# Reading the moving operand of split float32 products from the last column to the first, in a two-layer decoder trunk

## The chip, the cores and the metric

The kernel runs on one core of a Trainium2 chip. The metric is device time in microseconds; each number for a kernel is the median of several runs. Before the change: 1374.74 us, median of 3 runs (1374.43 to 1375.49).

## The reference

What is computed is a decoder trunk of two residual layers on 256 tokens of width 1024, all in float32:

```python
# layer 0
p = rms_norm(x) @ w_in_ab                 # 1024 x 2816
x = x + concat([gmlp(p), dilated_attention(p)]) @ w_out_ab
x = x + swiglu(rms_norm(x), ffn_w_gate, ffn_w_up, ffn_w_down)      # width 2816
# layer 1
p = rms_norm(x) @ w_in_cd                 # 1024 x 3072
x = x + concat([moba_attention(p), short_conv(p)]) @ w_out_cd
# 8 experts of width 3584; each token has two of them
h = rms_norm(x)
x = x + sum(gate[..., e] * (silu(h @ wg[e]) * (h @ wu[e])) @ wd[e] for e in range(8))
```

Nearly all of the arithmetic is in the products with the weight matrices: the projections, the dense feed-forward and the eight experts.

## The kernel before, in words

**Split products.** TensorE multiplies operands of the type `float32r`, a rounded float32. To keep more of the precision, every operand of a large product is split into two such parts: hi is the rounded value, lo is the remainder, rounded too. A product is then three matmuls into the same PSUM bank: hi x hi, hi x lo and lo x hi. The helper `three` (lines 786 to 790) issues them. Its arguments are the output in PSUM, the stationary operand (`sh`, `sl`: hi and lo) and the moving operand (`mh_`, `ml_`). TensorE first loads the stationary operand (128 x 128) and then streams the columns of the moving operand through the array, one after the other, and each gives one column of the result.

**Weights.** A stream of weight tiles of 2 MB comes from HBM into a ring of seven slots (`raw_ring`), loaded by SyncE's queue. Each tile is worked on in four units of 128 x 1024 values. For a unit ScalarE makes the hi part (`w_hi`, lines 402 and 423), VectorE makes the lo part (`w_lo`, lines 410 and 428), and TensorE uses both. There are four buffers for units (`SPLITS`). The semaphores `hi_ready`, `lo_ready` and `unit_used` count units: ScalarE waits for TensorE to have used a unit four before, VectorE waits for ScalarE, and TensorE waits for VectorE.

**Order of the work.** Every engine's program is written out by hand in order. TensorE's begins with the projection of layer 0 (`first_tile`, `project`), then attention with the output projection (`attention`, `ab_unit`), the dense feed-forward (`ffn`, `down`), the projection and the attention of layer 1 (`project`, `c_attention`, `conv_half`, `out_first`, `out_units`, `out_last`), the routing, and then the experts in `job`. A job is one expert on up to 128 gathered tokens: 21 steps of a gate, an up or a down tile, each of four units, and each unit is six matmuls of 512 columns. The first job stands alone, and the others are the passes of a loop.

**The two shapes.** In most places the activations are stationary and the weights move: the moving operand is a row of `w_hi` or `w_lo` of 512 columns (256 where a tile is narrower), and the output is a whole bank or half of one. In the dense feed-forward from its second slab on, and in the convolution (`conv_half`), the weights are stationary and 256 columns of activations (`ffn_in_hi`, `act_hi` and their lo parts) move.

Transposes, the small attention products and the gathers of tokens call TensorE directly and don't go through the helper.

Of the kernel before, what the change touches and what calls it, by code (L numbers as in the profile page):

```python
# [174 lines left out]
def decoder_trunk(nc, x, norm_mix, norm_ffn, w_in_ab, gmlp_v_gain, gmlp_ws, gmlp_bs, dil_q_gain, dil_k_gain,  # L175
# [10 lines left out]
    with ExitStack() as ctx:  # L186
# [4 lines left out]
        def at(name, shape, dt, offset):  # L191
            return nc.alloc_sbuf_tensor_at(name, [P, *shape], dt, offset=offset)
# [77 lines left out]
        mh = at("moe_h", [2, SLAB], F32, R0 + 12288)  # L270
# [111 lines left out]
        def raw_unit(u):  # L382
            t, r0, n, c0, w = units[u]
            _, nrow, ncol = tiles[t]
            full = raw[:, t % RING, 0:nrow * ncol].rearrange("p (k f) -> p k f", f=ncol)
            return full[:, r0:r0 + n, c0:c0 + w]
# [4 lines left out]
        def split_hi(act, u):  # L391

            if u >= U_MOE:
                return
            t, _, _, _, w = units[u]
            if u < 3:
                act.wait_ge(quarter_loaded[u], 16)
            else:
                act.wait_ge(slot_loaded[t % RING], 16 * (t // RING + 1))
            if u >= SPLITS:  # L400
                act.wait_ge(unit_used, u - SPLITS + 1)
            act.activation(part(wh, u, w), raw_unit(u), ACT.Copy).then_inc(hi_ready, 1)  # L402
# [380 lines left out]

        @block.tensor
        def _(pe):
            def three(out_, sh, sl, mh_, ml_, start, stop):

                pe.matmul(out_, sh, mh_, start=start, stop=False)  # L788
                pe.matmul(out_, sh, ml_, start=False, stop=False)  # L789
                return pe.matmul(out_, sl, mh_, start=False, stop=stop)  # L790

            def setup_mix():
                pe.wait_ge(ident_loaded, 16)
# [30 lines left out]
            def first_tile(n, u0, later_rows):  # L824

                for tt in range(TT):
                    sl = slice(tt * P, tt * P + P)
                    for i in range(4):
                        u = u0 + i
                        _, r0, cnt, _, w = units[u]  # L830
                        if tt == 0:
                            pe.wait_ge(lo_ready, u + 1)
                        pe.wait_ge(xt_lo, 8 * n + 4 * tt + i + 1)
                        for r in range(cnt):
                            k = r0 + r
                            mm = three(ps[:, tt, 0:w], in_hi[n][:, k, sl], in_lo[n][:, k, sl],
                                       part(wh, u, w)[:, r, :], part(wl, u, w)[:, r, :], k == 0, k == KD - 1)
                        if tt == 1:
                            mm.then_inc(unit_used, 1)
                        if tt == 0 and i == later_rows:  # L840
                            x_T(n, 1, 0)
                            x_T(n, 1, 1)
# [7 lines left out]
            def project(u0, u1, layer, c0=0):  # L850

                u, c = u0, c0
                while u < u1:
                    t = units[u][0]
                    ncol = tiles[t][2]
                    b = (c % 2) * 2
                    if c == 1 and layer == 0:
                        setup_columns()
                        setup_rows()
                        setup_ws()  # L860
                    if c == 2 and layer == 1:
                        spread_scale(2)
                    if c >= 2:
                        pe.wait_ge(proj_act, read_act[layer][c - 2])
                    while u < u1 and units[u][0] == t:
                        _, r0, n, _, w = units[u]
                        pe.wait_ge(lo_ready, u + 1)
                        for r in range(n):
                            k = r0 + r
                            for tt in range(TT):  # L870
                                sl = slice(tt * P, tt * P + P)
                                mm = three(ps[:, b + tt, 0:ncol], act_hi[:, k, sl], act_lo[:, k, sl],
                                           part(wh, u, w)[:, r, :], part(wl, u, w)[:, r, :], k == 0, k == KD - 1)
                        mm.then_inc(unit_used, 1)
                        u += 1
                    c += 1
# [190 lines left out]
            def conv_half(n):  # L1067

                i, half = divmod(n, 2)
                z, c = divmod(i, 2)  # L1070
                u = first["conv"] + i
                if half == 0:
                    pe.wait_ge(lo_ready, u + 1)
                    if i == 0:
                        pe.wait_ge(proj_act, 11)
                    if i == 4:
                        pe.wait_ge(cv_z, 1)
                o = ps[:, CONV_BANK[z], c * SEQ:(c + 1) * SEQ]
                for k in range(4 * half, 4 * half + 4):
                    mm = three(o, part(wh, u, P)[:, k, :], part(wl, u, P)[:, k, :],  # L1080
                               act_hi[:, k, :], act_lo[:, k, :], k == 0, k == KD - 1)
                if half == 1:
                    mm.then_inc(unit_used, 1)
# [328 lines left out]
            for half in range(2):  # L1412
# [5 lines left out]
                for t in range(TT):  # L1418
                    pe.matmul(bank(QUARTER_BANKS[half * TT + t]), pick_t[:, t, :], y_lo[:, cs],
                              start=False, stop=True).then_inc(last_done, 1)  # L1420
# [1191 lines left out]
```

## Time and profile before

| what | value |
|---|---|
| median of 3 runs | 1374.74 us |
| span of the profiled execution | 1372.6 us |
| TensorE busy | 1354.2 us, 6885 matmuls |
| TensorE weight loads | 1139.1 us, beside the matmuls |
| VectorE busy | 1180.1 us |
| ScalarE busy | 1017.8 us |
| moved by DMA | 430.89 MB |

The profiled execution is one of its own. Its time is given as the span, from its first to its last instruction; the medians of the runs also hold what lies around that. A matmul's row in the trace begins when it begins to stream and ends when its last result is modelled to have arrived, so rows of matmuls that follow each other overlap, and the time that one takes from the next is the distance between their starts. The granted clock (PEclk) is the share of TensorE's full clock of 2.4 GHz: 1.00 is that level, 0.50 would be 1.2 GHz.

### The profile page before, as it was taken

What the parts mean: (1) busy time and instruction counts of PE and PEld (TensorE: products, weight loads), DVE (VectorE), ACT (ScalarE), POOL (GpSimd) and SP (SyncE); (2) the same over time, 40 slices, a digit from 0 to 9 for tenths busy, and PEclk for the clock granted to TensorE, in tenths of its full rate; (3) what the DMA queues carried; (4) which work ended last, traced back from release to release, by engine and by line L of the source; (5) the groups of instructions that cost most, each with busy time, mean ns of one, the idle gap of its engine ahead of it and who ended that gap; (6) DMA issues with size and microseconds to landing.
All of it is one profiled execution on the core that took longest, in us unless ns stands there. A gap on an engine that the chain in (4) does not pass through costs nothing.

```text
span 1372.6 us, 19885 instructions
## 1 busy us (share of the span) xinstructions
PE 1354.2 (99%) x6885; PEld 1139.1 (83%) x6885; DVE 1180.1 (86%) x1369; ACT 1017.8 (74%) x1189; POOL 133.2 (10%) x132
## 2 busy tenths in 40 slices
PE   9999999999998999999999999999999999999998
PEld 7778999988987788888888888888888888888886
DVE  5876555568959999999999999999999999999998
ACT  5656444456757778888888888888888888888886
POOL 1020000000222240200200110020020002003000
PEclk9999999999999999999999999999999999999999
DMA  9944543643656999999999999999999999999980
GB/s 346 361 144 162 184 154 123 229 139 123 246 217 254 363 373 372 383 395 375 369 394 397 354 391 398 369 372 394 392 354 391 400 368 371 395 387 356 394 335 31
DMA packets 184623, 430.89 MB, mean 314 GB/s; under 512 B 6076, under 2 KB 14032, under 8 KB 184576
## 3 DMA queue, kind: packets, MB, share of 16 engines
q1 hardware_dynamic: 181136, 422.81, 82.8%
q0 software_dynamic: 3440, 7.44, 2.5%
q8 instruction: 30, 0.49, 0.1%
q14 instruction: 17, 0.14, 0.0%
HBM read 425.68 MB, written 7.36 MB: 315 GB/s over the span
## 4 chain that ended last, share of the span: by engine, by line
PE 90%; DVE 6%; DMA 1%; issue 1%; ACT 1%; POOL 0%; DVEq 0%; SPq 0%; POOLq 0%; ACTq 0%
PE psum L788 29%; PE psum L790 28%; PE psum L789 28%; DVE w_lo L428 2%; PE psum L1360 2%; DVE w_lo L410 1%; DMA slot_table<-routing,table_row 1%; DMA routing<-slot_table 0%; PE psum L820 0%; PE psum L921 0%; POOL slot_table L712 0%; DVE probs L2114 0%; PE psum L1062 0%; DMA const<-const_f 0%; PE psum L953 0%
## 5 line engine op out<-in xcount | busy, mean ns | idle before, releaser
L428 DVE TENSOR_TENSOR w_lo<-raw_ring,w_hi 128x1024 fp32r<-128x1024 f32 x674 | 811.2, 1228 | 49.0 <-ACT w_hi L423 12.1
L423 ACT ACTIVATE w_hi<-raw_ring 128x1024 fp32r<-128x1024 f32 x675 | 713.1, 1062 | 169.3 <-PE psum L790 168.4
L788 PE MATMUL psum<-w_hi,xg_hi 128*128 128x512 f32 x896 | 351.4, 392 | 4.2 <-DVE w_lo L428 4.1
L790 PE MATMUL psum<-w_hi,xg_lo 128*128 128x512 f32 x896 | 349.0, 390 | 0.0
L789 PE MATMUL psum<-w_lo,xg_hi 128*128 128x512 f32 x896 | 348.7, 389 | 0.0
L410 DVE TENSOR_TENSOR w_lo<-raw_ring,w_hi 128x1024 fp32r<-128x1024 f32 x124 | 151.3, 1227 | 78.0 <-ACT w_hi L402 77.1
L788 PEld LDWEIGHTS psum<-w_hi,xg_hi 128*128 128x128 f32 x896 | 168.2, 188 | 40.0 <-DVE w_lo L428 4.1
L402 ACT ACTIVATE w_hi<-raw_ring 128x1024 fp32r<-128x1024 f32 x124 | 130.0, 1058 | 93.9 <-PE psum L790 93.6
L790 PEld LDWEIGHTS psum<-w_hi,xg_lo 128*128 128x128 f32 x896 | 168.2, 188 | 35.4
L789 PEld LDWEIGHTS psum<-w_lo,xg_hi 128*128 128x128 f32 x896 | 168.3, 188 | 34.1
L788 PE MATMUL psum<-w_hi,moe_hT_hi 128*128 128x512 f32 x448 | 175.7, 392 | 0.7 <-DVE w_lo L428 0.7
L790 PE MATMUL psum<-w_hi,moe_hT_lo 128*128 128x512 f32 x448 | 174.5, 390 | 0.0
L789 PE MATMUL psum<-w_lo,moe_hT_hi 128*128 128x512 f32 x448 | 174.4, 389 | 0.0
L788 PEld LDWEIGHTS psum<-w_hi,moe_hT_hi 128*128 128x128 f32 x448 | 84.1, 188 | 19.8 <-issue 1.4
L790 PEld LDWEIGHTS psum<-w_hi,moe_hT_lo 128*128 128x128 f32 x448 | 84.1, 188 | 17.8
L789 PEld LDWEIGHTS psum<-w_lo,moe_hT_hi 128*128 128x128 f32 x448 | 84.1, 188 | 16.9
L788 PE MATMUL psum<-w_hi,act_hi 128*128 128x512 f32 (+1 forms) x224 | 86.0, 384 | 2.9 <-DVE w_lo L410 1.9
L789 PE MATMUL psum<-w_lo,act_hi 128*128 128x512 f32 (+1 forms) x224 | 83.9, 375 | 0.0
L790 PE MATMUL psum<-w_hi,act_lo 128*128 128x512 f32 (+1 forms) x224 | 83.9, 375 | 0.0
L788 PE MATMUL psum<-ffn_in_hi,w_hi 128*128 128x256 f32 x288 | 80.9, 281 | 0.0
L789 PE MATMUL psum<-ffn_in_lo,w_hi 128*128 128x256 f32 x288 | 80.6, 280 | 0.0
L790 PE MATMUL psum<-ffn_in_hi,w_lo 128*128 128x256 f32 x288 | 80.6, 280 | 0.0
(299 smaller groups left out, 1348.4 us busy)
## 6 DMA issues: line engine op xcount, KB each, us to landing
raw_ring<-in_moe_w_gate SPq DMA_DIRECT2D x56, 2048.0 KB, 10.4
raw_ring<-in_moe_w_up SPq DMA_DIRECT2D x56, 2048.0 KB, 11.0
raw_ring<-in_moe_w_down SPq DMA_DIRECT2D x56, 2048.0 KB, 10.1
raw_ring<-in_ffn_w_gate SPq DMA_DIRECT2D x5, 2048.0 KB, 12.5
raw_ring<-in_ffn_w_up SPq DMA_DIRECT2D x5, 2048.0 KB, 8.9
raw_ring<-in_ffn_w_down SPq DMA_DIRECT2D x5, 2048.0 KB, 10.3
raw_ring<-in_w_in_ab SPq DMA_DIRECT2D x4, 2048.0 KB, 19.4
raw_ring<-in_w_in_cd SPq DMA_DIRECT2D x4, 2048.0 KB, 8.0
```

Source lines behind the costliest of these rows:

```text
L402: act.activation(part(wh, u, w), raw_unit(u), ACT.Copy).then_inc(hi_ready, 1)
L410: dve.tensor_tensor(part(wl, u, w), raw_unit(u), part(wh, u, w).bitcast(F32), ALU.subtract).then_inc(lo_ready, 1)
L423: act.activation(wh[:, v % SPLITS, :], moe_raw(i, q), ACT.Copy).then_inc(hi_ready, 1)
L428: dve.tensor_tensor(wl[:, v % SPLITS, :], moe_raw(i, q), wh[:, v % SPLITS, :].bitcast(F32), ALU.subtract).then_inc(lo_ready, 1)
L788: pe.matmul(out_, sh, mh_, start=start, stop=False)
L789: pe.matmul(out_, sh, ml_, start=False, stop=False)
L790: return pe.matmul(out_, sl, mh_, start=False, stop=stop)
L1360: mm = pe.transpose(ps[:, 4 + n % 2, c * P:(c + 1) * P], mh[:, n % 2, c * P:(c + 1) * P], ident)
```

## The change

In the helper of the split products the output and both parts of the moving operand are turned: the access pattern begins at the last column and goes down by one column at a time. Column n of the moving operand still gives column n of the output, so the result is the same; only the order in which columns are read and written differs. The stationary operands are not touched.

```diff
+            def turned(v):
+
+                return v[:, v.shape[-1] - 1::-1]
+
             def three(out_, sh, sl, mh_, ml_, start, stop):
 
-                pe.matmul(out_, sh, mh_, start=start, stop=False)
-                pe.matmul(out_, sh, ml_, start=False, stop=False)
-                return pe.matmul(out_, sl, mh_, start=False, stop=stop)
+                o, mh, ml = turned(out_), turned(mh_), turned(ml_)
+                pe.matmul(o, sh, mh, start=start, stop=False)
+                pe.matmul(o, sh, ml, start=False, stop=False)
+                return pe.matmul(o, sl, mh, start=False, stop=stop)
```

The instructions of all five engines stand in the same order as before; after the change the helper's three matmuls are lines 793 to 795, and the lines below are five further on.

## Rows read from the trace of the kernel before

**Rows 1.** The page's head, busy time by engine, and its slices.

```profile
span 1372.6 us, 19885 instructions
PE 1354.2 (99%) x6885; PEld 1139.1 (83%) x6885; DVE 1180.1 (86%) x1369; ACT 1017.8 (74%) x1189; POOL 133.2 (10%) x132
...
PEclk9999999999999999999999999999999999999999
```

**Rows 2.** The page's chain that ended last, by engine and line.

```profile
PE 90%; DVE 6%; DMA 1%; issue 1%; ACT 1%; POOL 0%; DVEq 0%; SPq 0%; POOLq 0%; ACTq 0%
PE psum L788 29%; PE psum L790 28%; PE psum L789 28%; DVE w_lo L428 2%; PE psum L1360 2%; DVE w_lo L410 1%; DMA slot_table<-routing,table_row 1%; DMA routing<-slot_table 0%; PE psum L820 0%; PE psum L921 0%; POOL slot_table L712 0%; DVE probs L2114 0%; PE psum L1062 0%; DMA const<-const_f 0%; PE psum L953 0%
```

**Rows 3.** Busy time by engine in one pass of the expert loop.

```profile
core 0: us, PE busy (x) PEld busy (x) DVE busy (x) ACT busy (x) POOL busy (x), PEclk, DMA share, GB/s
754.41:871.97 117.56, 117.56 (x535) 97.40 (x533) 110.63 (x100) 96.74 (x99) 9.87 (x9) 1.00 1.03 382
```

**Rows 4.** Waits of TensorE: total us, times, longest; the first two.

```profile
PE psum L788 <- DVE w_lo L428: 4.8, 5, 1.7
PE psum L788 <- DVE w_lo L410: 1.9, 4, 0.6
```

**Rows 5.** TensorE's groups by form, line 788: busy us, mean ns.

```profile
L788 PE MATMUL psum<-w_hi,xg_hi 128*128 128x512 f32 x896 | 351.4, 392 | 4.2 <-DVE w_lo L428 4.1
...
L788 PE MATMUL psum<-w_hi,moe_hT_hi 128*128 128x512 f32 x448 | 175.7, 392 | 0.7 <-DVE w_lo L428 0.7
...
L788 PE MATMUL psum<-ffn_in_hi,w_hi 128*128 128x256 f32 x288 | 80.9, 281 | 0.0
...
L788 PE MATMUL psum<-w_hi,act_hi 128*128 128x512 f32 x192 | 76.7, 399 | 2.9 <-DVE w_lo L410 1.9 <-issue 0.8
...
L788 PE MATMUL psum<-w_hi,ffn_h_hi 128*128 128x512 f32 x88 | 34.4, 391 | 0.0
...
L788 PE MATMUL psum<-act_hi,w_hi 128*128 128x256 f32 x48 | 14.5, 303 | 0.2 <-ACT p_v L1709 0.2
...
L788 PE MATMUL psum<-w_hi,ffn_in_hi 128*128 128x512 f32 x32 | 12.8, 399 | 0.2 <-DVE ffn_in_lo L1916 0.2
...
L788 PE MATMUL psum<-w_hi,act_hi 128*128 128x256 f32 x32 | 9.3, 290 | 0.0
```

**Rows 6.** Timeline of TensorE in the experts, 512 columns: start us, us.

```profile
799.95 0.39 PE L788 MATMUL psum<-w_hi,xg_hi 128*128 128x512 f32 x1
...
804.02 0.39 PE L788 MATMUL psum<-w_hi,xg_hi 128*128 128x512 f32 x1
```

**Rows 7.** Timeline of TensorE in the dense feed-forward, 256 columns.

```profile
179.84 0.28 PE L788 MATMUL psum<-ffn_in_hi,w_hi 128*128 128x256 f32 x1
...
181.96 0.28 PE L788 MATMUL psum<-ffn_in_hi,w_hi 128*128 128x256 f32 x1
```

**Rows 8.** Line 1342: its rows in the timeline, and one's duration (min/median/max ns).

```profile
410.48 1.02 PE L1342 MATMUL psum<-const 128*128 128x512 f32 x2
...
L1342 PE MATMUL psum<-const x2: 592/594/595, 410.5 to 410.9; 128*128 128x512 f32 x2
```

## The prediction
> **What bounds the kernel now.** I read the head of the page first. TensorE is busy for 1354.2 of 1372.6 us and its granted clock is at full share in every slice, so the engine runs at the 2.4 GHz level from end to end [rows 1]. The profiled execution has its span alone as a time; the median of the three runs is 1374.74 us, 2.1 us above it, and I put those 2.1 us around the span both before and after. Next the chain of waits: 90% of it is TensorE, and 29 + 28 + 28 = 85% of the span lies on three lines, 788 to 790, which are the body of `three`, the helper that the change edits [rows 2]. Then I ask whether something else is close behind. In one pass of the expert loop (117.56 us) TensorE has no idle time; VectorE is busy for 110.63 us and ScalarE for 96.74 us [rows 3]. The longest waits of TensorE on the whole span are 4.8 and 1.9 us [rows 4]. So a matmul that gets slower lengthens the run almost one for one, and one that gets faster shortens it until VectorE's 110.63 us per pass is reached.
>
> How many matmuls does the edit touch, and at what pace do they run? The groups by form give the counts for line 788 [rows 5]; lines 789 and 790 have the same counts. With 512 columns: 896 + 448 + 192 + 88 + 32 = 1656 per line, 4968 on the three. With 256 columns: 288 + 48 + 32 = 368 per line, 1104 on the three. Together 6072 of the 6885 matmul rows. The mean of one in that view (392 ns) is not the pace, because a matmul's row overlaps the next one's. The pace is read from starts in the timeline: from 799.95 to 804.02 us there are 18 matmuls of 512 columns, so 4.07/18 = 0.2261 us each [rows 6]; from 179.84 to 181.96 us there are 18 of 256 columns, 2.12/18 = 0.1178 us each [rows 7]. The difference, 0.1083 us for 256 columns, is 0.423 ns per column, and one clock at 2.4 GHz is 0.417 ns. So a column goes through in one clock, and what is left is a fixed 0.2261 - 512 x 0.000423 = 9.5 ns per matmul. All in all 4968 x 0.2261 + 1104 x 0.1178 = 1123 + 130 = 1253 us, 91% of the span.
>
> **The change part by part.** It removes no instruction, adds none and moves none: each engine's program holds the same rows in the same order, and only the two operands' address patterns differ. The step from column to column becomes -1 and the start becomes the last column. The stationary operand is read as before, so weight loads stay as they are. Waits and signals sit on the same matmuls. Each output column still receives the same products in the same sequence of matmuls. A bank's reader still waits for the end of the last matmul of its group, so it does not matter to it which column was written last. Within a group every matmul is turned, so a given column is returned to one matmul later, as before. Work that does not go through the helper (transposes, attention products, gathers, 813 rows) is untouched. All these parts cost 0 us, and no cover is needed for any of them.
>
> What is left is one unknown: the price of stepping backwards, for the read of the moving operand and for the write of the result. No matmul of the kernel before has a negative step on either side, so I bound the price.
>
> *From above.* The nearest row in which TensorE takes more time per column is line 1342, a plain float32 product of 512 columns done in two passes. From its start at 410.48 us to the end of the second pass are 1.02 us, and one pass shows 0.594 us, so the second began 0.426 us after the first [rows 8]. That is 0.83 ns per column, two clocks instead of one at the same granted clock. If a backward step cost this, a product of 512 columns would take 0.426 - 0.2261 = 0.200 us more, and one of 256 (half of 0.426 is 0.213) 0.0952 us more: 4968 x 0.1999 + 1104 x 0.0952 = 993 + 105 = 1098 us.
>
> *From below.* The stream is already at one column per clock, so the columns themselves can't go faster. At most the fixed 9.5 ns could vanish: 6072 x 9.5 ns = 58 us. In one pass (21 steps of four units of six matmuls, 504) that would be 4.8 us, less than the 117.56 - 110.63 = 6.9 us by which VectorE is shorter, so VectorE would not stop it.
>
> Between ends so far apart I take 0. What the row of line 1342 has different is the kind of product (plain float32 in two passes), not the order of addresses: its operands are read forwards. The turned products are of the same kind, width and alignment as the rows at 0.2261 us; they touch the same bytes of the same banks, all of them and each once, and have the same number of columns per matmul. An even width turned round pairs the same neighbours: 511 with 510 instead of 510 with 511.
>
> The Trainium skill speaks on both sides here. "PSUM — Partial Sum Buffer", section Specifications (TRN2), says that PSUM has lines of 8 bytes and that any non-contiguous access pattern slows matmuls significantly. "SBUF — State Buffer", section on the DMA port swizzle, says that SBUF lines are 16 bytes and that consecutive accesses to the same line run at full bandwidth. If a step of -1 counts as non-contiguous, the first makes the sum the rival's below; if only staying in the line counts, it makes the sum 0, since two float32 columns share an 8-byte line and four share a 16-byte line in either direction. No run here shows yet which reading holds.
>
> The sum is 0 us on a median of 1374.74: I predict 1374.7 us. For this kernel, with three runs spread over 1.06 us, I call a difference under 0.2% (2.75 us) no change.
>
> **The rivals.** (1) *Backwards at half the rate.* TensorE streams two columns at a time only upwards, or merges pairs of writes only upwards, and falls to two clocks per column. The place is the moving read or the PSUM write of all 6072 matmuls, the price is the 1098 us above, and the time 1374.7 + 1098 = 2473 us. For it: line 1342 shows that the engine has such a rate [rows 8]. Against it: the same bytes, the same pairs. It decides as soon as a matmul costs 0.45 ns more (2.75 us over 6072), since TensorE has next to no slack [rows 3, 4]. Chance 0.09. (2) *A fixed price per matmul*, for instance a start in the middle of a line: between 0.45 ns and once more the fixed 9.5 ns, so up to 6072 x 9.5 ns = 58 us and at most 1432 us; one extra clock alone would be 2.5 us, or 1377.3. Nothing speaks for it but that the starting address is another one. Chance 0.05. (3) *Faster*: part of the fixed 9.5 ns goes, or the read meets the accesses of the other engines less often; 1317 us at the utmost. Against it: the pace is the same 0.2261 us while VectorE and ScalarE are busy for 94% and 82% of the time, and it is already one column per clock but for that remainder. Chance 0.03. (4) *The change doesn't reach the chip*, because the two reversals are folded into a forward pattern: the built program holds the step of -1 on both operands, so I give it no chance apart from the forecast's, with which it shares its time.
>
> **How the numbers follow.** Forecast 0.83, rivals 0.09, 0.05 and 0.03. Faster by over 0.2% is rival 3: 0.03. Slower by over 0.2% is rivals 1 and 2: 0.14. Within 0.2%: 0.83. The forecast's own band is 1372.0 to 1377.5 us. I carry the upper end to 1380, which takes in two extra clocks per matmul (6072 x 0.83 ns = 5.1 us), the cheap part of rival 2; rival 1 is left out, because nothing lies between.
>
> **What would show it.** If right: starts of consecutive 512-column products stay 0.226 us apart and those of 256 columns 0.118 us, the three lines of the helper keep about 85% of the chain, one pass of the expert loop stays at 117.6 us, and ScalarE still ends its waits on TensorE. If rival 1 holds, the starts are 0.43 us apart, VectorE's share falls to nearly half, and the loop's pass takes over 210 us. If rival 2 holds, both widths are longer by the same number of nanoseconds. A different spacing of the starts for 512 and 256 columns, or a granted clock below full share, would prove the argument wrong even at the same total.

## The result, and the profile after

The changed kernel takes 1402.82 us (median of 4 runs, 1402.51 to 1403.27) against 1374.59 us for the kernel before (median of 4, one more than before the prediction): ratio 1.0204, 95% interval 1.0189 to 1.0218. It is slower by 28.2 us. The forecast was no change, with a range up to 1380 us.

The head of the page of the changed kernel, its slices of the granted clock, and its chain by line:

```profile
span 1401.4 us, 19885 instructions
PE 1385.1 (99%) x6885; PEld 1142.2 (82%) x6885; DVE 1183.3 (84%) x1369; ACT 1017.6 (73%) x1189; POOL 118.6 (8%) x132
...
PEclk9999999999999999999999999999999999999999
...
PE psum L793 30%; PE psum L795 29%; PE psum L794 29%; PE psum L1365 2%; DVE w_lo L428 1%; DVE w_lo L410 1%; PE psum L825 0%; PE psum L1224 0%; PE psum L926 0%; DVE probs L2119 0%; PE psum L1067 0%; PE psum L958 0%; DVE rope_tmp L480 0%; DVE p_qk L482 0%; PE psum L1218 0%
```

Against [rows 1, 2]: the same instructions, the same clock, the same three lines on the chain. TensorE is busy for 30.9 us more (1385.1 - 1354.2), and its idle time falls from 18.4 to 16.3 us, since some waits for VectorE shrink: 30.9 - 2.1 = 28.8 us, the growth of the span. One pass of the expert loop, the counterpart of [rows 3]:

```profile
core 0: us, PE busy (x) PEld busy (x) DVE busy (x) ACT busy (x) POOL busy (x), PEclk, DMA share, GB/s
646.52:767.21 120.69, 120.69 (x534) 97.63 (x533) 111.01 (x100) 96.70 (x99) 8.63 (x9) 1.00 1.01 372
```

It is 3.13 us longer, 6.2 ns for each of its 504 products. VectorE and ScalarE need what they needed. The starts of products in TensorE's timeline, as in [rows 6, 7], first the 512 columns of the experts, then the 256 columns of the dense feed-forward:

```profile
822.45 0.40 PE L793 MATMUL psum<-w_hi,xg_hi 128*128 128x512 f32 x1
...
826.65 0.40 PE L793 MATMUL psum<-w_hi,moe_hT_hi 128*128 128x512 f32 x1
...
179.92 0.28 PE L793 MATMUL psum<-ffn_in_hi,w_hi 128*128 128x256 f32 x1
...
182.04 0.28 PE L793 MATMUL psum<-ffn_in_hi,w_hi 128*128 128x256 f32 x1
```

Between each pair lie 18 products: 4.20/18 = 0.2333 us with 512 columns (0.2261 before), and 2.12/18 = 0.1178 us with 256 (0.1178 before). These two windows alone would say 7.2 ns for 512 columns; the pass averages over 504 products, and I go by its 6.2 ns. So the whole price lies on the 4968 products of 512 columns, and at 6.2 ns each it is 30.8 us.

### The profile page after: what moved, and what is told of

The parts are those of the page before. It is cut to its first block, busy times and chain, and to the rows that moved or that the text cites. A ratio compares the mean times of both kernels' runs of the same rounds, so it can differ in the third digit from the quotient of the medians.

```text
span 1401.4 us, 19885 instructions
## 1 busy us (share of the span) xinstructions
PE 1385.1 (99%) x6885; PEld 1142.2 (82%) x6885; DVE 1183.3 (84%) x1369; ACT 1017.6 (73%) x1189; POOL 118.6 (8%) x132
## 4 chain that ended last, share of the span: by engine, by line
PE 93%; DVE 5%; ACT 1%; issue 1%; DVEq 0%; ACTq 0%
PE psum L793 30%; PE psum L795 29%; PE psum L794 29%; PE psum L1365 2%; DVE w_lo L428 1%; DVE w_lo L410 1%; PE psum L825 0%; PE psum L1224 0%; PE psum L926 0%; DVE probs L2119 0%; PE psum L1067 0%; PE psum L958 0%; DVE rope_tmp L480 0%; DVE p_qk L482 0%; PE psum L1218 0%
## 5 line engine op out<-in xcount | busy, mean ns | idle before, releaser
L793 PE MATMUL psum<-w_hi,xg_hi 128*128 128x512 f32 x896 | 358.4, 400 | 3.7 <-DVE w_lo L428 3.6
L794 PE MATMUL psum<-w_lo,xg_hi 128*128 128x512 f32 x896 | 356.2, 398 | 0.0
L795 PE MATMUL psum<-w_hi,xg_lo 128*128 128x512 f32 x896 | 356.0, 397 | 0.0
L793 PE MATMUL psum<-w_hi,moe_hT_hi 128*128 128x512 f32 x448 | 178.8, 399 | 0.1
L795 PE MATMUL psum<-w_hi,moe_hT_lo 128*128 128x512 f32 x448 | 178.0, 397 | 0.0
L794 PE MATMUL psum<-w_lo,moe_hT_hi 128*128 128x512 f32 x448 | 178.0, 397 | 0.0
```

The costliest lines, as they stand in the source:

```text
L793: pe.matmul(o, sh, mh, start=start, stop=False)
L794: pe.matmul(o, sh, ml, start=False, stop=False)
L795: return pe.matmul(o, sl, mh, start=False, stop=stop)
```

## The experiments

Five of the twelve runs are tables of extra products: rows of 24 matmuls of one kind, on a source line each, behind the last matmul of the kernel before, while the other engines rest (VectorE's last products and the last transfers end within the first row). They write PSUM banks that nobody reads any more. What counts there is the distance between starts within a row; I give it as the start of the next row minus the start of this one, over 24. Their whole times (1475 to 1499 us) say nothing.

### Read or write, and which width

```diff
...
+            for n in R:
+                pe.matmul(o5, wt, m5, start=n == 0, stop=n == 23)
+            for n in R:
+                pe.matmul(back(o5), wt, back(m5), start=n == 0, stop=n == 23)
+            for n in R:
+                pe.matmul(o5, wt, back(m5), start=n == 0, stop=n == 23)
+            for n in R:
+                pe.matmul(back(o5), wt, m5, start=n == 0, stop=n == 23)
...
```

> The kernel before with rows of 24 extra products behind its last matmul (they write PSUM banks whose contents are not needed any more), so the time grows by some 110 us and only the distance between starts within each row counts. In the kernels before and after that distance is 226.7 and 233.3 ns for 512 columns, and 117 and 118 ns for 256. Theory 1, the READ of the moving operand backwards costs time per column: both turned and read turned give 233 at 512 columns, write turned alone 227; 384 columns get 5 ns longer and 256 columns 3 ns unless something else (the weight load) already holds 256 columns at 117. Theory 2, the WRITE to PSUM backwards costs time: both and write turned give 233, read turned alone 227. Theory 3, a fixed price per matmul at its start: +6.6 ns at every width that is not held by the weight load, so 384 columns too. Theory 4, the moving reads meet the reads of the next weight load, which is done beside them: the price shrinks with the number of stationary columns, so with 64 or 32 of them both directions fall towards 213 ns (512 columns at one per clock) and their difference vanishes; under theories 1 to 3 it stays. If the other engines' accesses were the cause, the directions would not differ here, since they rest. Single products without accumulation and two alternating banks: no change under any of these. Reads that start at column 1 or 2 tell whether the start within a line matters.

The timeline of the extra rows (start us, us in all, line). Line 1431 reads and writes 512 columns forwards, 1433 turns both, 1435 the read alone, 1437 the write alone; 1439 and 1441 are 384 columns, 1443 and 1445 are 256, forwards and with both turned:

```profile
1368.11 5.60 PE L1431 MATMUL psum<-moe_y_hi,pick_T 128*128 128x512 f32 x24
1373.55 5.77 PE L1433 MATMUL psum<-moe_y_hi,pick_T 128*128 128x512 f32 x24
1379.15 5.76 PE L1435 MATMUL psum<-moe_y_hi,pick_T 128*128 128x512 f32 x24
1384.75 5.62 PE L1437 MATMUL psum<-moe_y_hi,pick_T 128*128 128x512 f32 x24
1390.21 4.35 PE L1439 MATMUL psum<-moe_y_hi,pick_T 128*128 128x384 f32 x24
1394.40 4.42 PE L1441 MATMUL psum<-moe_y_hi,pick_T 128*128 128x384 f32 x24
1398.66 3.04 PE L1443 MATMUL psum<-moe_y_hi,pick_T 128*128 128x256 f32 x24
1401.54 3.01 PE L1445 MATMUL psum<-moe_y_hi,pick_T 128*128 128x256 f32 x24
1404.38 5.63 PE L1447 MATMUL psum<-moe_y_hi,pick_T 128*128 128x512 f32 x24
```

Forwards (1373.55 - 1368.11)/24 = 226.7 ns, both turned 233.3, read turned 233.3, write turned 227.5. So it is the read. 384 columns: 174.6 and 177.5; 256 columns: 120.0 and 118.3. The two numbers of the kernel come back with the other engines at rest, so they have no part in it. Products that don't accumulate, further down in the table, gave 227.9 and 233.3, so accumulation has none either. Theories 2 and 3 fall. Theory 4 in its plain form falls as well: with 64 and 32 stationary columns the forward rows took 230.0 and 231.3 and the backward ones 233.8 and 233.3, no nearer to 213. One thing fitted nothing: forward reads from column 1 and 2 took 237.5 and 233.3 ns, as slow as backward ones.

### Widths, starts and order in blocks

The same frame with other rows: more widths, other first columns, and the 512 columns in blocks of 4, 16 or 256.

```diff
...
+                pe.matmul(o4, wt, by4[:, 127::-1, :], start=n == 0, stop=n == 23)
...
+                pe.matmul(o4, wt, by4[:, :, 3::-1], start=n == 0, stop=n == 23)
...
```

> The kernel before with rows of 24 extra products behind its last matmul; only the distance between starts within a row counts. All write forwards except where a block pattern says so. Theory A (the backward read has a slower rate): 227.7, 174.5, 120.0 ns forwards and 233.3, 177.6, 118.7 backwards for 512, 384, 256 columns lie on lines of 0.42 ns per column + 13 and 0.45 + 4. So 448 columns: 200 and 205; 320: 147 and 148; 192 and 128: 93 and 67 forwards, 90 and 61 backwards, or the floor of a weight load (about 109) if that is longer, and then no difference. Theory B (a fixed price at the first column of a backward read, which 256 columns hide behind the weight load): 448 and 320 columns both get 6.6 ns longer. Start of a read: a forward read from column 2 took 233.2, from column 1 237.7; if lines of 16 bytes matter, 4, 8 and 16 are back at 227 and 3 is not; if 32 or 64 bytes matter, only 8 or 16 are. Backward from 515, 519 or 527 shows the same from the other end (233 or better). Blocks: if the order of the lines costs, blocks of 4 or 16 columns read from the last block to the first, each forwards, take 233 and blocks in order that are turned inside take 227; if the order inside a line costs, the other way round.

Lines 1441 and 1443 are 320 columns forwards and backwards; 1453 and 1455 are 512 columns forwards from column 8 and 16; 1467 reads blocks of 4 columns from the last to the first, 1469 blocks in order but each turned inside:

```profile
1378.51 3.71 PE L1441 MATMUL psum<-moe_y_hi,pick_T 128*128 128x320 f32 x24
1382.06 3.69 PE L1443 MATMUL psum<-moe_y_hi,pick_T 128*128 128x320 f32 x24
1385.58 5.04 PE L1445 MATMUL psum<-moe_y_hi,pick_T 128*128 128x448 f32 x24
...
1406.48 5.76 PE L1453 MATMUL psum<-moe_y_hi,pick_T 128*128 128x512 f32 x24
1412.08 5.67 PE L1455 MATMUL psum<-moe_y_hi,pick_T 128*128 128x512 f32 x24
1417.59 6.00 PE L1457 MATMUL psum<-moe_y_hi,pick_T 128*128 128x512 f32 x24
...
1445.91 5.76 PE L1467 MATMUL psum<-moe_y_hi,pick_T 128*128 128x512 f32 x24
1451.51 5.63 PE L1469 MATMUL psum<-moe_y_hi,pick_T 128*128 128x512 f32 x24
1456.97 5.76 PE L1471 MATMUL psum<-moe_y_hi,pick_T 128*128 128x512 f32 x24
```

| columns | 128 | 192 | 256 | 320 | 384 | 448 | 512 |
|---|---|---|---|---|---|---|---|
| forwards, ns | 109.6 | 113.3 | 120.0 | 147.9 | 174.6 | 203.3 | 226.7 |
| backwards, ns | 111.3 | 111.3 | 118.3 | 146.7 | 177.5 | 206.7 | 233.3 |

(256, 384 and 512 are from the first table, where both operands are turned.) Up to 320 columns the two directions differ by about 2 ns at most, now one way and now the other; at 384 and 448 backwards costs about 3 ns and at 512 it costs 6.6. That is neither a slower rate per column nor a fixed price, so theory A and theory B are both wrong in form. Blocks of 4 columns (16 bytes) in reverse order cost the full price, 233.3; the same blocks in order but turned inside cost nothing, 227.5. So it is the order in which the 16-byte pieces follow each other that counts, not the order inside one. Two blocks of 256 in reverse order, each read forwards, took 228.8: one step back in the middle costs next to nothing. Blocks of 16 turned inside were the slowest of the rows in blocks, 266.7. A read that alternates between forwards and backwards from one product to the next took 236.3, and one backwards from column 514 took 242.9; the runs leave both unexplained. And forward reads that start 8 columns on took 233.3, from 16 on 229.6: the *place* of a forward read matters as much as the direction.

### In the kernel: only 256 columns, only the read, only the write

```diff
...
+                if out_.shape[-1] == 256:
+                    out_, mh_, ml_ = turned(out_), turned(mh_), turned(ml_)
```

> The helper turns its operands only where the output has 256 columns (1104 of 6072 matmuls). Theory A (slower rate, with 256 columns held by something else, as the 120.0 and 118.7 ns of the extra rows show): no change, 1374 to 1376 us. Theory B (a fixed price per matmul): 1104 x 6.6 ns = 7.3 us more, 1382 us.

Measured 1375.27 us (ratio 1.0005, interval 0.9995 to 1.0014): no change, as the table of widths says.

For the next two, the gate and up products of the experts alone are touched, and the two readers of their banks read backwards, so that the result stays right:

```diff
...
-                                mm = three(bank(b), xg_hi[:, k, :], xg_lo[:, k, :], wh[:, w % SPLITS, cs],
-                                           wl[:, w % SPLITS, cs], k == 0, k == KD - 1)
+                                mm = three(bank(b), xg_hi[:, k, :], xg_lo[:, k, :], turned(wh[:, w % SPLITS, cs]),
+                                           turned(wl[:, w % SPLITS, cs]), k == 0, k == KD - 1)
...
-                        act.activation(msg[:, i % 2, :], bank(i % 2), ACT.Silu).then_inc(silu_ready, 1)
+                        act.activation(msg[:, i % 2, :], bank(i % 2)[:, 511::-1], ACT.Silu).then_inc(silu_ready, 1)
...
-                dve.tensor_tensor(mh[:, i % 2, :], msg[:, i % 2, :], bank(2 + i % 2), ALU.mult).then_inc(h_ready, 1)
+                dve.tensor_tensor(mh[:, i % 2, :], msg[:, i % 2, :], bank(2 + i % 2)[:, 511::-1], ALU.mult).then_inc(h_ready, 1)
```

> Only the experts' gate and up products (2688 matmuls of 512 columns), and only the moving operand read backwards; the bank is written forwards, so it holds the columns in reverse, and the two readers (ScalarE's silu, VectorE's product) read it backwards. Theory A (the read is what costs): 2688 x 6.6 ns = 17.7 us more, 1392 us. Rival (the write costs in the loaded loop): no change, 1375 us.

Measured 1390.52 us (ratio 1.0117, interval 1.0100 to 1.0134), 16.0 us more, against 2688 x 6.2 = 16.7 us at the price per product of the result. TensorE's timeline where a down step, read forwards, goes over into a gate step, read backwards:

```profile
820.43 0.39 PE L792 MATMUL psum<-w_hi,moe_hT_hi 128*128 128x512 f32 x1
...
822.47 0.40 PE L792 MATMUL psum<-w_hi,xg_hi 128*128 128x512 f32 x1
...
824.57 0.40 PE L792 MATMUL psum<-w_hi,xg_hi 128*128 128x512 f32 x1
```

Nine products lie between each two: (822.47 - 820.43)/9 = 226.7 ns, then (824.57 - 822.47)/9 = 233.3 ns.

With `turned(bank(b))` in place of the two `turned(wh...)` and `turned(wl...)`:

> The same gate and up products, but only the output is written backwards; the moving operand is read forwards, and the same two readers read the bank backwards. Theory A: no change, 1374 to 1376 us. Rival (the write costs in the loaded loop): 1392 us. If the readers' reversed reads cost ScalarE or VectorE time, this and the run with the backward read show it alike in the mean durations of the silu and of the product (680 ns before).

Measured 1374.65 us (ratio 1.0000, interval 0.9991 to 1.0010). Writing backwards is free, in the loaded loop too. Reading a bank backwards is free for ScalarE and VectorE: the product of silu and up took 681 ns in the mean, as against 680 before, and the silu 579 as against 581.

### The place of the stationary operand

The forward reads with another start left a new question. In every table the stationary operand stayed where it was while the moving one went on. Now the stationary operand moves within its buffer `y_lo`. Its place is the column of `y_lo` at which it begins; `y_lo` itself begins 12288 bytes, 48 x 256, behind `y_hi`, so place 0 is a multiple of 256 bytes from the moving operand's first column:

```diff
...
+                pe.matmul(o5, y_lo[:, 8:136], y_hi[:, 0:512], start=n == 0, stop=n == 23)
...
+                pe.matmul(o5, y_lo[:, 8:136], back(y_hi[:, 0:512]), start=n == 0, stop=n == 23)
...
```

> The kernel before with rows of 24 extra products of 512 columns behind its last matmul, all written forwards. So far the extra rows with the stationary operand in one place gave 227 (forwards from column 0), 233 (backwards from column 511), and forwards from column 2, 4, 8, 16: 233.2, 231.8, 233.2, 229.3, so a forward read can cost as much as a backward one. Theory C: the moving read and the read of the next stationary operand, which goes on beside it, meet in SBUF, and what counts is where one lies against the other and in which directions they go. Then moving the stationary operand alone, by 2 to 128 columns, changes the forward pace from 227 in the same way (231 to 235 for some), a common shift of both by 4, 8 or 16 columns gives 227 again, and the backward pace varies with it too and is 227 or so for some place. Theory D: the moving read alone sets the pace, by its own start and direction. Then moving the stationary operand changes nothing (227 forwards, 233 backwards in every row), a common shift keeps 231.8, 233.2 and 229.3, and shifts of the moving read by 32 to 256 columns are 227 or slightly more.

Lines 1428 and 1430 have the stationary operand at place 0, 1440 and 1442 at 8, 1452 at 64 columns (the first of each pair reads forwards); 1462 has both operands 8 columns on:

```profile
1368.61 5.60 PE L1428 MATMUL psum<-moe_y_hi,moe_y_lo 128*128 128x512 f32 x24
1374.05 5.77 PE L1430 MATMUL psum<-moe_y_hi,moe_y_lo 128*128 128x512 f32 x24
1379.66 5.71 PE L1432 MATMUL psum<-moe_y_hi,moe_y_lo 128*128 128x512 f32 x24
...
1402.01 5.75 PE L1440 MATMUL psum<-moe_y_hi,moe_y_lo 128*128 128x512 f32 x24
1407.60 5.77 PE L1442 MATMUL psum<-moe_y_hi,moe_y_lo 128*128 128x512 f32 x24
1413.20 5.77 PE L1444 MATMUL psum<-moe_y_hi,moe_y_lo 128*128 128x512 f32 x24
...
1435.68 5.62 PE L1452 MATMUL psum<-moe_y_hi,moe_y_lo 128*128 128x512 f32 x24
1441.13 5.77 PE L1454 MATMUL psum<-moe_y_hi,moe_y_lo 128*128 128x512 f32 x24
...
1463.36 5.63 PE L1462 MATMUL psum<-moe_y_hi,moe_y_lo 128*128 128x512 f32 x24
1468.82 5.63 PE L1464 MATMUL psum<-moe_y_hi,moe_y_lo 128*128 128x512 f32 x24
```

The same forward read takes 226.7 ns with the stationary operand at place 0, 232.9 at place 8, 227.1 at place 64, and 227.5 when both go 8 columns on. Backwards: 233.8, 233.3, 233.3. Theory D falls: the place of the stationary operand sets the pace of a forward read. The load of the stationary operand takes 188 to 189 ns on average in every row of this table, so it is not the load that gets longer. A common shift by 4 columns gave 231.7 where theory C wanted 227, so the rule is not exact below 8 columns.

The remaining places, with two runs of whole kernels beside them:

> The remaining places of the stationary operand in steps of 4 columns (12, 20 to 28, 36 to 60; a shift of 64 gave the same as 0), each with the moving operand read forwards and backwards, 512 columns, behind the last matmul of the kernel before. Theory C, in the form that forwards and backwards each have good and bad places: forwards 229 to 234 except near 0 or 64, backwards 227 or so for at least one place that has not been tried. Theory C2, the backward read meets the stationary read wherever that lies, because both go down through the columns: backwards 233 to 237 everywhere. A place with less than 226.7 in either direction would be one that beats both kernels.

| place of the stationary operand, columns | 0 | 2 | 4 | 8 | 12 | 16 | 20 | 24 | 28 |
|---|---|---|---|---|---|---|---|---|---|
| forwards, ns | 226.7 | 230.8 | 233.3 | 232.9 | 233.3 | 233.8 | 232.1 | 233.8 | 233.3 |
| **place** | **32** | **36** | **40** | **44** | **48** | **52** | **56** | **60** | **64** |
| forwards, ns | 232.5 | 232.9 | 232.9 | 230.4 | 228.8 | 232.1 | 233.3 | 227.9 | 227.1 |

Backwards every place gave 233 to 234, but for 32 and 36, with 236.7 and 237.1. So theory C missed for the backward read: no place tried is a good one. The numbers are those of C2, but its reason is not shown by them, and no run reads the stationary operand in the opposite order, which would test it. For a forward read 0, 60 and 64 are good places. No row was below 226.7, so nothing here beats the kernel before.

The two kernels move the buffers R0 and R1, which hold the stationary operands of the experts, the projections and the down products, by 32 bytes (the constant `PHASE` is added to their address); the moving ones, `w_hi` and `w_lo`, stay:

```diff
-PHASE, FFN_PHASE = 32, -64
+PHASE, FFN_PHASE = 64, -64
```

> The changed kernel with the buffers of activations (the stationary operands of the projections, the experts and the down products) 32 bytes, 8 columns, further on, and the moving ones where they were. The extra rows gave 233.4 ns backwards with this shift and 233.5 without. Theories C and C2: no change against the changed kernel, 1402 to 1404 us. Theory D (the direction alone sets the pace): the same.

The changed kernel with the shift: 1402.95 us, ratio to the kernel before 1.0207 (1.0190 to 1.0224), as without it.

> The kernel before with the same shift of the stationary buffers by 32 bytes; everything is read and written forwards. Theory C: forward products of 512 columns fall to the 233 ns that this shift gave in the extra rows (227 without), so 4968 x 6.3 ns = 31 us less some waits that go, 1400 to 1405 us, as slow as the changed kernel without turning anything. Theory D (direction alone): no change, 1374 to 1376 us.

The kernel before with the shift, nothing turned: 1402.86 us, ratio 1.0209 (1.0192 to 1.0226). It is as slow as the changed kernel. One pass of its expert loop, and its largest group by form:

```profile
646.26:766.88 120.62, 120.62 (x534) 97.54 (x533) 110.94 (x100) 96.77 (x99) 8.53 (x9) 1.00 1.02 374
...
L788 PE MATMUL psum<-w_hi,xg_hi 128*128 128x512 f32 x896 | 356.9, 398 | 3.8 <-DVE w_lo L428 3.7
```

120.62 us for a pass against 117.56 in [rows 3] and 120.69 in the changed kernel. Two more shifts, by `PHASE` of 288 (256 bytes) and of 96 (64 bytes), test the period:

> The kernel before with its buffers of activations 256 bytes (64 columns) further on, all read and written forwards. Theory C (for a forward read only the place of the stationary operand against the moving one counts, and places repeat after 64 columns, as the extra rows with 64 and 128 gave 227.3 and 227.7): no change against the kernel before, 1373 to 1376 us. Rival (any shift of these buffers costs time, through the other engines or by chance): about 1403 us, as with 32 bytes.

> The same with 64 bytes (16 columns). Theory C: the extra row with a shift of 16 columns gave 233.8 ns forwards, 227 without a shift: 1402 to 1406 us. Rival (what counts is the alignment of each buffer to 64 bytes by itself): no change, 1375 us.

256 bytes: 1374.58 us (ratio 0.9999, 0.9989 to 1.0008). 64 bytes: 1404.21 us (ratio 1.0214, 1.0197 to 1.0231). Both as theory C has it. In the kernel before, `w_hi` begins at byte 131200 of each partition and R0 at 186752; the difference, 55552, is 217 x 256, so nearly all of its large products stand at place 0.

The exception is a check within one run. The 96 products of 512 columns with `ffn_in_hi` and `ffn_in_lo` as stationary operands have them 64 bytes below R0 (`FFN_PHASE`), at place 48. The shift by 64 bytes takes these to place 0 and the others to 16. In that run's timeline they alone keep the fast pace, (134.25 - 130.16)/18 = 227.2 ns, while the experts' products take (826.20 - 822.00)/18 = 233.3 ns:

```profile
130.16 0.39 PE L788 MATMUL psum<-w_hi,ffn_in_hi 128*128 128x512 f32 x1
...
134.25 0.39 PE L788 MATMUL psum<-w_hi,ffn_in_hi 128*128 128x512 f32 x1
...
822.00 0.40 PE L788 MATMUL psum<-w_hi,xg_hi 128*128 128x512 f32 x1
...
826.20 0.40 PE L788 MATMUL psum<-w_hi,moe_hT_hi 128*128 128x512 f32 x1
```

### A shorter stationary operand

```diff
...
+                pe.matmul(ps[0:2, 0, 0:512], y_lo[:, 0:2], y_hi[:, 0:512], start=n == 0, stop=n == 23)
...
```

> Extra rows of 24 products behind the last matmul, now with 2 to 96 stationary columns. If what the backward read lacks is a good meeting with the read of the next stationary operand, that read has to matter less as it gets shorter: with 2 or 8 stationary columns both directions and both places (0 and 8 columns further on) come out alike, within 1 ns, at 227 or below, down to 213 if it is all of what lies over one column per clock; with 96 the difference is about that of 128 (227 and 233). Rival: the direction itself or the place costs whatever the length of the stationary read; then 2 columns still show 227 and 233. With 128 stationary columns in the bad place (8 further on): 384 moving columns take about 177 in both directions (173 to 174 forwards in the good place), and 256 columns 118 to 120 in both, which is why those widths showed little or nothing.

Lines 1427 and 1429 have 2 stationary columns, 1447 and 1449 have 96, forwards and backwards:

```profile
1369.22 5.66 PE L1427 MATMUL psum<-moe_y_hi,moe_y_lo 128*2 128x512 f32 x24
1374.71 5.77 PE L1429 MATMUL psum<-moe_y_hi,moe_y_lo 128*2 128x512 f32 x24
1380.32 5.73 PE L1431 MATMUL psum<-moe_y_hi,moe_y_lo 128*8 128x512 f32 x24
...
1424.88 5.69 PE L1447 MATMUL psum<-moe_y_hi,moe_y_lo 128*96 128x512 f32 x24
1430.41 5.77 PE L1449 MATMUL psum<-moe_y_hi,moe_y_lo 128*96 128x512 f32 x24
1436.02 5.72 PE L1451 MATMUL psum<-moe_y_hi,moe_y_lo 128*2 128x512 f32 x24
```

Two columns: 228.8 forwards, 233.8 backwards; 96 columns: 230.4 and 233.8. The expectation missed: a shorter read of the stationary operand does not bring the directions together, and forwards it even loses part of the advantage. With 32 stationary columns at place 8 a forward read took 238.8, more than the backward one beside it (233.8). With 128 stationary columns in the bad place (8), 384 moving columns took 173.8 forwards, no worse than in the good one, and 256 took 118.3. So the place matters at 512 columns and not at these two widths. That the two reads meet in SBUF, as theory C has it, is not shown: what the runs show is that order and place set the pace, and by what mechanism stays open.

## Why the prediction was wrong

**What bounds the kernel: right.** TensorE without slack, the three lines of the helper on the chain, and a full granted clock [rows 1 to 4] all came back in the changed kernel, and the 30.8 us of the products reached the end but for some 2 us of waits.

**That nothing else moves: right.** Same instructions, same busy time of VectorE per pass (110.63 and 111.01 us), and the write side is free (227.5 ns, 1374.65 us).

**The step that failed** is the choice between the bounds: "Between ends so far apart I take 0", on the ground that the turned products touch the same bytes in the same pairs. That counts bytes and leaves out the order in which they are read: blocks of 4 columns in reverse order cost the full price, the same blocks turned inside cost nothing. It also took the rows at 0.2261 us [rows 6] for the rate of a forward read as such. They are the rate of a forward read whose stationary operand lies a multiple of 256 bytes from it; at the other places tried the same read takes 228 to 234 ns, the shifted kernel before takes 1402.86 us, and a backward read has no place among those tried where it does better than 233. The change took that advantage away; by what mechanism the order and the place act is open. The price is 6.2 ns per product of 512 columns, 30.8 us, between my two ends of -58 and +1098 us but far from where I put it.

**A second step was weak:** the split of the pace into 0.423 ns per column and a fixed 9.5 ns, drawn through two widths [rows 6, 7]. In the table of widths 128 and 192 columns cost about the same (110 and 113 ns), and from 320 to 512 columns the line is (226.7 - 147.9)/192 = 0.41 ns per column with 226.7 - 512 x 0.417 = 13 ns left. The products of 256 columns showed no loss when they were turned, and a line through both widths could not show that one of them is insensitive.

**The rivals.** Half the rate was wrong by a factor of about 35 (1098 us forecast, 31 measured). The fixed price per matmul had a span of 1377.5 to 1432 us that holds 1402.8, but its mechanism is wrong: by it both widths had to lengthen by the same time, and 256 columns did not lengthen. The prediction named the sign that would prove it wrong, a different change for 512 and 256 columns, and that is what came.

**The rules of the pages.** The Trainium skill's "PSUM — Partial Sum Buffer", section Specifications (TRN2), warns of non-contiguous access patterns of matmuls; a step of -1 in PSUM cost nothing here (227.5 against 226.7 ns). The 16-byte lines in the Trainium skill's "SBUF — State Buffer" agree with the blocks of 4 columns, which are free when they are turned inside (227.5 ns); in reverse order they are not (233.3). So of the two readings in the prediction neither held: the output's step was free, and staying in the line was not enough for the moving read. The Trainium skill's "TensorE: Matmul & The Clock Gate", section "Step-by-step: what each phase is for", says that the moving operand and the weight load have independent read ports, so that a load takes nothing from the running matmul. For these products the measurement does not agree, and it decides: moving the stationary operand alone by 8 columns took the same moving read from 226.7 to 232.9 ns.

## What to carry to other kernels

A matmul pace read from a trace holds for its operands' addresses as well as for its shape: when an edit moves a buffer or turns an access pattern of a stream that bounds the kernel, price it by a table of such products with the place and the direction varied, not by the pace of the present one. On a kernel bound by `float32r` products of 512 columns, lay the stationary operands a multiple of 256 bytes from the moving ones within a partition and read forwards; here that is worth 2%. Outputs of 512 columns can be written, and banks read by ScalarE and VectorE, in either direction at no cost that these runs show.

## What was not expected of the hardware

The 226.7 ns of a forward product and the 233.3 ns of a backward one are the same within 1 ns whether the other engines are at work or at rest. A moving operand of every second column takes twice the time (450.8 ns forwards, 466.3 backwards, in the first table). Blocks of 16 columns turned inside take 266.7 ns, longer than the whole turned round. And the whole loss of 28.2 us can be had without turning anything, by moving some buffers 32 bytes.
